# Recurrent heads of a two-block network: TensorE, ScalarE, VectorE and GpSimd each walk an order of their own

## The reference

```
qkv = silu(conv(h @ w_in[:, :3072]))                 # 5 taps, per channel
q, k = l2norm(q) * 128**-0.5, l2norm(k)
a_kk = strict(kb @ k.T * gam)                        # kb = k * beta
u, w = solve(a_kk + I, [v * beta, kb * exp(g)])      # unit lower triangular
per chunk: v_new = u - w @ S
           o = (q * exp(g)) @ S + a_qk @ v_new
           S = S * exp(g_last) + (k * exp(g_last - g)).T @ v_new
o = rmsnorm(o_f + o_b, norm_a) * silu(z)
```

## Time and profile before

| | |
|---|---|
| median of 3 executions | 3232.31 us (3230.91 to 3233.63) |
| profiled execution | 3229.48 us, span 3227.7 us |
| TensorE matmul busy | 3070.5 us, 95% |
| VectorE, ScalarE, GpSimd busy | 1564.5, 1078.8, 380.3 us |
| granted TensorE clock, mean | 0.976 |
| recurrent halves | 120 to 1060 us, with TensorE busy 888 |

### The profile page before, as it was taken

One profiled execution on the slowest core, in us unless ns is written; L12 is line 12 of the kernel. 1 busy time (PEld: TensorE's weight loads), 2 busy tenths in 40 slices (PEclk: granted clock), 3 DMA queues, 4 the chain that ended last, 5 costly groups with the idle time before them and its releaser, 6 DMA issues.

```text
span 3227.7 us, 39047 instructions
## 1 busy us (share of the span) xinstructions
PE 3070.5 (95%) x16271; PEld 2553.9 (79%) x16271; DVE 1564.5 (48%) x2182; ACT 1078.8 (33%) x2304; POOL 380.3 (12%) x436
## 2 busy tenths in 40 slices
PE   7999999999989999999999999999999999997998
PEld 4788888877878877887878788888888877876887
DVE  4455556566564224132147554444444669532453
ACT  3443443444443213232332341111221334213453
POOL 0122222222231000000001100000000012001111
PEclk9999999999999999999999999999999989997999
DMA  2211111011012111111252321111111321111001
GB/s 109 67 49 50 40 53 46 34 40 33 27 37 65 46 56 47 50 40 49 109 211 105 115 96 59 53 40 53 52 40 53 107 73 52 53 39 46 27 27 40
DMA packets 59362, 192.77 MB, mean 60 GB/s; under 512 B 7697, under 2 KB 15377, under 8 KB 49970
## 3 DMA queue, kind: packets, MB, share of 16 engines
q1 hardware_dynamic: 58320, 189.19, 17.0%
q10 hardware_dynamic: 866, 1.09, 0.1%
HBM read 156.28 MB, written 33.98 MB: 59 GB/s over the span
## 4 chain that ended last, share of the span: by engine, by line
PE 85%; DVE 9%; ACT 3%; issue 2%; POOL 0%; DMA 0%; ACTq 0%; DVEq 0%; POOLq 0%
PE ps L2447 22%; PE ps L2449 21%; PE ps L2448 21%; PE ps L704 3%; PE ps L710 3%; PE ps L1703 2%; PE ps L3291 1%; DVE ar L1111 1%; PE ps L747 1%; PE ps L741 1%; PE ps L3350 1%; PE ps L756 1%; PE ps L755 1%; PE ps L1668 1%; DVE ar L1211 1%
## 5 line engine op out<-in xcount | busy, mean ns | idle before, releaser
L2447 PE MATMUL ps<-r,r 128*128 128x512 f32 (+2 forms) x2976 | 1182.9, 397 | 47.4 <-DVE r L232 13.6
L2449 PE MATMUL ps<-r,r 128*128 128x512 f32 (+2 forms) x2976 | 1123.0, 377 | 0.0
L2448 PE MATMUL ps<-r,r 128*128 128x512 f32 (+2 forms) x2976 | 1120.5, 377 | 0.0
L2447 PEld LDWEIGHTS ps<-r,r 128*128 128x128 f32 x2976 | 567.3, 191 | 149.2 <-issue 23.8
L2449 PEld LDWEIGHTS ps<-r,r 128*128 128x128 f32 x2976 | 564.8, 190 | 106.5
L2448 PEld LDWEIGHTS ps<-r,r 128*128 128x128 f32 x2976 | 568.0, 191 | 86.3 <-issue 4.1
L2447 PE MATMUL ps<-r 128*128 128x512 f32 x512 | 199.7, 390 | 0.8 <-DVE r L2440 0.8
L2449 PE MATMUL ps<-r 128*128 128x512 f32 x512 | 199.3, 389 | 0.0
L2448 PE MATMUL ps<-r 128*128 128x512 f32 x512 | 199.2, 389 | 0.0
L2697 DVE TENSOR_TENSOR ar<-ar,ps 128x512 f32<-128x512 f32 x224 | 151.3, 686 | 92.5 <-PE ps L2449 92.1
L2435 ACT ACTIVATE r<-ar 128x2048 fp32r<-128x2048 f32 x48 | 91.6, 1909 | 260.8 <-PE ps L2449 254.4
(11 more groups left out here) (326 smaller groups left out, 4014.4 us busy)
## 6 DMA issues: line engine op xcount, KB each, us to landing
ar<-wst SPq DMA_DIRECT2D x72, 1024.0 KB, 4.9
ar<-wst SPq DMA_DIRECT2D x56, 512.0 KB, 3.8
ar<-x SPq DMA_DIRECT2D x16, 512.0 KB, 5.3
ar<-sc_g SPq DMA_DIRECT2D x32, 256.0 KB, 4.8
sc_h<-ar SPq DMA_DIRECT2D x32, 256.0 KB, 2.2
sc_x<-ar SPq DMA_DIRECT2D x16, 512.0 KB, 2.8
ar<-sc_x SPq DMA_DIRECT2D x16, 512.0 KB, 4.3
sc_b<-ar SPq DMA_DIRECT2D x24, 260.0 KB, 2.0
```

What stands on the lines that cost most here:

```text
L2447: t.do.matmul(o, l[0], r[0], start=first, stop=False)
L2448: t.do.matmul(o, l[0], r[1], start=False, stop=False)
L2449: return t.do.matmul(o, l[1], r[0], start=False, stop=last)
```

## The change

A table LEANS adds, for an engine, a kind of half and a part, small numbers to the a and b of some threads; the function `leaning` merges them anew for each engine. Engines walk their own lists in halves 0 to 15. The opening and the last list stay common, GpSimd's table is empty, and SP still walks `plan`. Each engine executes the same instructions as before.

```
--- before.py
+++ after.py
@@ -487,7 +487,19 @@
 
 
         NPREP, NINV, NSCAN, NFIN = 16, 21, 3, 4
+        LEANS = {
+            "pe": {("fill", 0): {"scan": (-0.02, 0.0)}, ("fill", 1): {"inv": (0.03, 0.0)}, ("gate", 0): {"inv": (0.0, 0.01)}, ("gate", 1): {"inv": (0.03, 0.0), "scan": (0.0, -0.04)}, ("plain", 0): {"scan": (-0.01, 0.0), "inv": (-0.02, 0.02)}, ("plain", 1): {"scan": (0.0, -0.03), "inv": (0.01, 0.0)}},
+            "act": {("gate", 0): {"prep0": (-0.02, -0.02)}, ("plain", 1): {"inv": (0.0, 0.02)}},
+            "dve": {("fill", 0): {"scan": (-0.01, 0.0)}, ("fill", 1): {"inv": (0.04, 0.0), "fin": (0.02, 0.0)}, ("gate", 0): {"scan": (0.0, -0.01), "prep0": (-0.03, 0.0), "inv": (0.0, 0.02)}, ("gate", 1): {"prep1": (-0.03, 0.02)}, ("plain", 0): {"prep0": (0.01, 0.0), "scan": (0.0, -0.02)}, ("plain", 1): {"prep1": (0.01, 0.0), "inv": (0.0, 0.01), "scan": (0.0, 0.04)}},
+            "pool": {},
+        }
+
+        def leaning(engine, s, threads):
+            by = LEANS[engine].get(("fill" if s >= 14 else "gate" if s // 2 + 1 in GATES else "plain", s % 2), {})
+            return merged(*[(k, n, a_ + by.get(k[0], (0.0, 0.0))[0], b_ + by.get(k[0], (0.0, 0.0))[1]) for k, n, a_, b_ in threads])
+
         plan = [merged((("prep", 0), 4 * NPREP, 0.0, 1.0), (("gates",), 14, 0.15, 0.75), (("bias",), 13, 0.3, 1.0))]
+        plans = {engine: list(plan) for engine in LEANS}
         for s in range(16):
             h, part = divmod(s, 2)
             threads = [(("inv", h, part), NINV, 0.0, 1.0)]
@@ -504,8 +516,12 @@
             else:
                 threads.append((("fill", 8 + part), 32, 0.0, 1.0))
             plan.append(merged(*threads))
+            for engine in plans:
+                plans[engine].append(leaning(engine, s, threads))
 
         plan.append(merged((("scan", 7, 2, 8), 6 * NSCAN, 0.0, 0.3), (("fin", 7), NFIN, 0.32, 0.5), (("qk", 0), 33, 0.0, 1.0), (("split",), 1, 0.6, 0.8)))
+        for engine in plans:
+            plans[engine].append(plan[-1])
 
         def col(n, c, d, h):
 
@@ -794,7 +810,7 @@
                     return both(pe_prep0(t, 0), pe_prep1(t, 0))
                 return {"gates": pe_gates, "prep0": pe_prep0, "prep1": pe_prep1, "inv": pe_inv, "scan": pe_scan, "fin": pe_fin, "bias": pe_bias, "qk": pe_qk, "fill": pe_fill, "split": lambda t: idle(1), "dec": lambda t, *_: idle(3)}[what](t, *of)
 
-            for order in plan:
+            for order in plans["pe"]:
                 walk(order, make)
 
 
@@ -1052,7 +1068,7 @@
                     return halved(both(act_prep0(a, 0), act_prep1(a, 0)))
                 return {"gates": act_gates, "prep0": lambda a, h: halved(act_prep0(a, h)), "prep1": lambda a, h: halved(act_prep1(a, h)), "inv": act_inv, "scan": act_scan, "fin": act_fin, "bias": act_bias, "qk": act_qk, "fill": lambda a, h: halved(act_fill(a, h)), "split": act_first_split, "dec": act_dec}[what](a, *of)
 
-            for order in plan:
+            for order in plans["act"]:
                 walk(order, make)
 
 
@@ -1272,7 +1288,7 @@
                     return idle(1)
                 return {"qk": dve_qk0, "fill": lambda v, h: halved(dve_fill(v, h)), "gates": dve_gates, "prep0": lambda v, h: halved(dve_prep0(v, h)), "prep1": lambda v, h: halved(dve_prep1(v, h)), "inv": dve_inv, "scan": dve_scan, "fin": dve_fin, "split": dve_first_split, "dec": lambda v, *_: idle(3)}[what](v, *of)
 
-            for order in plan:
+            for order in plans["dve"]:
                 walk(order, make)
 
 
@@ -1355,7 +1371,7 @@
                     return halved(both(idle(NPREP), pool_prep1(p, 0)))
                 return idle(1) if what in ("gates", "prep0", "bias", "qk", "fill", "split") else {"prep1": lambda p, h: halved(pool_prep1(p, h)), "inv": pool_inv, "dec": pool_dec, "scan": pool_scan, "fin": pool_fin}[what](p, *of)
 
-            for order in plan:
+            for order in plans["pool"]:
                 walk(order, make)
```

## The result

The changed kernel takes 3173.55 us (median of four executions, 3173.29 to 3173.99), the kernel before beside it 3232.2 us. The ratio is 0.9819, with a 95% interval of 0.9802 to 0.9836.

What follows compares the result with a forecast made beforehand. TensorE's stops bound the kernel (85% of the chain; 93 us of waits as ceiling). Terms 4.0 + 10.8 + 12.3 + 12.2 + 4.2 = 43.5 us, cut to 33, gave 3199 us against 3232.3; range 3183 to 3223.

Steps and rivals of the forecast that it cites:

- I keep three quarters, 33 us, by choice: Halves 0 to 15: of 43.5 us of summed waits only 33 us come, since later partners may prove late too.
- The clock is no term: About 120 to 1060 us: clock averages 0.99; 1.2 GHz stretches total at most 19 us, cost at most 9.
- Rival 1: All halves: the whole 43.5 us comes, with some clock, giving 3189 us or a little less; chance 0.16.
- Fill: Halves 14 and 15: fewer waits, 2.8 us in half 14 and an estimated 1.4 in half 15; 4.2 us.
- gate part 0: Halves 0, 2, 4, 6: one more projection before Y5, scan's X2 ahead of the level 1 copy; 4.0 us.
- plain part 1: Halves 9, 11, 13: Y1, Y2, Y5 and others wait less, Yb copy costs 0.6; 4.05 each, 12.2 us.
- plain part 0: Halves 8, 10, 12: Y1, the scan's w steps and Y5 wait less; 4.1 us each, 12.3 us.
- Gate part 1: Halves 1, 3, 5, 7: L232 ahead of L1211, Y5 and Y1 covered, some given back at Y2; net 10.8 us.
- Rival 2: Halves with the finish: GpSimd's L1341 still starts before VectorE's copy L1211 and holds it; 5 us less gain, 3204; chance 0.15.
- Rival 3: All sixteen halves: covered waits return at the next inversion block, 19 us more than counted; 3218 us; chance 0.11.
- Rival 4: All halves: no change, inversion round trips and VectorE's queue set a half's length; 3232 us; chance 0.08.
- Rival 5: Fourteen convolution halves: VectorE, ScalarE and TensorE wait in a ring, at least 3.3 us each, 46 us; slower, 3235; chance 0.06.

Runs made afterwards that it cites:

- ScalarE alone: The changed kernel with TensorE's and VectorE's leanings emptied, so only ScalarE walks a list of its own: 3238.8 us, ratio 1.0029 to the kernel before.
- TensorE with VectorE: The changed kernel with ScalarE's leanings emptied, so ScalarE walks the common list: 3180.1 us, ratio 0.9837 to the kernel before.
- the changed one shifted: The changed kernel with the first bias product issued three times in the opening, so the halves begin later: 3175.1 us, ratio 0.9829 to the kernel before.
- the two shifted ones: The kernel before and the changed kernel, each with two extra bias products in the opening: 3231.8 and 3175.1 us.
- the reversed race: The changed kernel with VectorE's first finish step ahead of a convolution step in halves 9, 11, 13, so GpSimd's product starts before VectorE's masked copy: 3182.4 us.
- VectorE alone: The changed kernel with TensorE's and ScalarE's leanings emptied, so only VectorE walks a list of its own: 3202.4 us, ratio 0.9911 to the kernel before.

## Why the prediction was wrong

**"I keep three quarters, 33 us, by choice": the step that failed.** The sum of the listed waits, 43.5 us, was right to 2 us: the stops gave 43.9 + 1.8 = 45.7. The quarter that I took off stood for waits that come back at the next partner. They do come back when one engine moves alone (7.1 us lost, or 3.6 won of the roughly 20 that the same steps are worth in company). They did not here, because all three orders moved together and the partners moved with the stop. I had priced each wait with all engines' new orders, so this effect was, as I read it, already in the sum, and the discount took it off a second time. That the sum held is measured; that this is the reason rests on the kernels with one engine's order. The misfit of 25 us is made up, to within 0.3, of 10.5 for the discount, 9.6 for the clock (below), 2.2 that the sum was short, 0.6 left over and 2.8 that I had added because the profile of before lay under its median, which the changed kernel's does not.

**"The clock is no term": the other one.** Five stretches in the halves went, at 1.6 us each, and a longer one in the opening, worth 1.6 us between the two profiles: 9.6 us. The last has nothing to do with the change. My own bound was right ("cost at most 9" for the 19 us of low clock; the twins give 8 for 17 us), and I used it for the low end only. 45.7 + 9.6 + 0.6 left over = 55.9. Rival 1, the whole sum with "some clock", was the true case; its 3189 was too high because it held no figure for the clock.

**The terms, by the lengths less their stretches.** Gate halves: 14.8 forecast, 17.6 measured in the kernel with gate halves alone. Plain halves: 24.5, against 23.4 in the one with plain halves alone. Fill: 4.2, against 2.9 + 1.8. By the wait lists the split inside them was less good, and errors of either sign cancel: gate part 0 gave 7.3 us for the 4.0 forecast and plain part 1 17.1 for 12.2, but plain part 0 only 9.0 for 12.3. That the sum came within 2 us is in part luck.

- Gate part 0: I had 1.0 a half, and the list fell from 2.4 to 0.5, since the level 0 copies' 0.7 went too, which I had left out.
- Gate part 1: 2.7 a half, measured 3.2 in three of them (4.6 to 1.4). L232's 10.1 us went whole. The 0.9 given back at Y2 came as 0.7.
- Plain part 0: 4.1 a half forecast, 3.0 measured (7.0 to 4.0). Y1 and the scan's w came as worked out (2.3 to 1.0, 1.5 to 0). Y5 did not: I took L1111 to leave, and its place was taken by the convolution step one later, L1127 at 726.14. It kept 1.3 of its 1.6 us. A flip that waits 0.5 for L1133 was not in my working.
- Plain part 1: 4.05 forecast, 5.7 measured (10.7 to 5.0). The race was won as forecast, and VectorE's order alone wins it too. The 0.6 for ScalarE's Yb copy was not paid: X5 and XT5 have no stop in half 11, and XT4 has one of 0.4.

**The rivals.** Rival 2 (the race) was wrong in the plain halves and right in gate part 1, where I had counted it so. Rival 3 gave the right mechanism for one engine alone and the wrong one for the change. Rival 4 has nothing left: halves 0 to 14 shortened by 43.9 us, where their waits fell by 48.1. Rival 5 (a ring) shows on ScalarE alone, at 7.1 us and not 46, because the other engines stand still only until the transposes are made.

**The signs named.** The list fell to 43.9, not 60; L232 fell below 2, L1228's below 5, L1215's and L1194's by half and by 61% in place of a third; L1000's stayed; the part behind the halves kept its length to 0.6 us. The masked copy's longest in plain part 1 fell to 1.70 us and not to 1.3: at level 1, where the race was, it is 1.33, and the 1.70 is a copy of level 3 that overlaps another GpSimd instruction (L1311). Beside that one the new order also lost a little that I had not looked for: the level 1 copy takes 1.72 us in halves 2, 4 and 6 (1.32 before) and 2.40 in half 1 (1.52 before).

**Left open.** What the clock does outside the halves was not tried. Two kernels whose order there is the same, TensorE with VectorE and the changed one shifted, take 2224.0 and 2230.8 us from the KQ of half 15 to the end of their profiles, with 110.7 and 134.5 us of it at 1.2 GHz, and single runs of one kernel scatter by 12 to 15 us.

## What to carry to other kernels

Where each engine runs its own fixed order, price a reordering by the waits that it covers and then keep the sum, if the orders of all engines that meet there move together; that rests on this one case. Take a discount for moves of one engine alone, and look for what they can lose: of the three here two won 3.6 and 19.6 us of stops and one lost 7.1. Test such a change by stage (here by half), where gains added, and not by engine, where they didn't. Look for the stops of an experiment as far as its edit reaches, not only in the stretch that you have watched so far. And when the matmul engine's stops are what goes, read twin stages with and without a fall of its clock, and put the fall into the sum as a term of its own.

## What the runs showed of the hardware

- **The clock falls in the same work or not, from profile to profile.** The opening up to half 0 has the same order in all kernels. 97 to 106 us, before and changed, by the table by stretch:

```profile
97.00:106.00 9.00, 8.77 (x20) 5.03 (x21) 5.00 (x11) 1.12 (x4) 2.66 (x1) 0.62 0.41 117
```
```profile
97.00:106.00 9.00, 7.82 (x29) 5.19 (x30) 5.91 (x12) 2.07 (x11) 2.66 (x1) 1.00 0.45 115
```

  TensorE had stood still for 2 us before it in both. Of the fourteen profiles five have this fall, and their half 0 begins at 120.7 to 121.3 us (the two shifted ones at 122.9); the nine others begin at 117.9 to 119.1. The Trainium skill, TensorE: Matmul & The Clock Gate, "Part 1: The HAM clock gate (the "warmup" mystery)", says that the activity is judged in windows that run free of the kernel's start, so that one kernel may differ from run to run. The two rows, and the changed kernel's runs from 3166.0 to 3177.7 us, fit this; no row shows the windows themselves.
- **A small stop can cost more than itself.** 4.1 us of stops, put back by the reversed race, brought two falls of the clock worth 3.2 us in the profile, and a median about 9 us higher (three runs). It need not: VectorE alone, with 74.6 us of waits, has no fall in its halves.
- **Who starts first, by 0.3 us, decides 1.4 us.** VectorE's masked copy of 128x512 took 1.33 us when it was 0.93 us ahead of GpSimd's 128x1024 product, and 2.74 to 2.76 when it was 0.31 to 0.37 us behind. With no GpSimd instruction beside it the same copy of level 1 took 1.30 us in half 10, so the 1.33 is the time unheld.
